# Every second column of the MLP's first weights as a stationary tile, and the second weights' rows to match

## The chip, the cores and the metric

The kernel runs on one core of one Trainium2 chip. The metric is the device time of one execution in microseconds (us), and the three runs shown are compared by their median.

## What is computed

The reference is a decoder trunk of four layers on 256 tokens with 1024 features, in float32. Each layer has a token mixer (latent attention, block-sparse attention, a state-space mixer, latent attention again) and then a dense MLP with a squared ReLU. The part that matters here is the MLP:

```python
def sq_relu_mlp(h, w1, w2):
    a = jax.nn.relu(h @ w1)
    return (a * a) @ w2

for i in range(DEPTH):
    ...
    x = x + m
    x = x + sq_relu_mlp(rmsnorm(x, norm_mlp[i]), mlp_w1[i], mlp_w2[i])
```

`mlp_w1[i]` is 1024 x 4096 and `mlp_w2[i]` is 4096 x 1024. The sum over the 4096 hidden channels does not depend on the order in which they are taken, as long as a column of w1 and a row of w2 with the same number meet.

## The kernel before

All products run on TensorE with each float32 operand split into a high and a low part (`whi`, `wlo` for weights; `hhi`, `hlo` for activations; `uhi`, `ulo` for the hidden values), and three of the four cross products are summed in PSUM. Weights come in units of up to 1 MB, in the order of a list that `plan_mlp` and its sisters write (`units`). SP goes through that list (L2186 to L2203): it waits until the slot's last low split is done, and starts the transfer into one of four slots of `raw`. ScalarE copies a landed unit to `whi` (L557) once TensorE has released the slot; VectorE subtracts to get `wlo` (L573); TensorE waits for that before it uses the unit.

An MLP takes its 4096 hidden channels in 16 chunks of 256. Chunk c has a first-layer unit ("up", columns 256c to 256c+255 of w1, as 8 slabs k of 128 features x 256 columns) and a second-layer unit ("down", rows 256c to 256c+255 of w2, as 2 slabs of 128 rows x 1024 columns). The function `cols` cuts the first, the function `rows` the second; in `rows`, slab k holds the rows 128k to 128k+127 of the unit, one row to a partition.

In the first layer the weights are stationary: a tile m (0 or 1) of 128 hidden channels is loaded for each k, and the 256 tokens are the moving operand. The result lands in PSUM with hidden channels on the partitions. Chunks 0 and 1 of an MLP go through `pe_first_channels` (L841 to L894), with its own high-part loop `first_part` (L855, L856, L861) and the three-product helper `mm3` (L590 to L592). That function also serves the state-space mixer, with keys "dt" and ("cv", 0); `deferred(j)` tells an MLP. Chunks 2 to 15 go through `pe_up` (L974 to L989): for each tile m and each k one product of the high weights with high and low activations side by side (512 moving columns, L982), then for each m and k one product of the low weights with the high activations (256 moving columns, L987).

ScalarE and VectorE turn the PSUM tile into relu, square and its high and low parts (L1027, L1048, L1050, L1032, L1053), always on 128 x 512 elements and element by element. In the second layer the hidden values are stationary, 128 channels of tile k against 128 tokens, and the rows of the down unit's slab k are the moving operand (`pe_out_part`, L902, L903, L906): 24 products of 512 columns for each chunk. Thus slab k of the down unit and tile m = k of the up unit must hold the same channels on the same partitions. TensorE's order is written out in `pe_mlp`: down(c-2), then up(c).

Of the kernel before, what the change touches and what calls it, by code (L numbers as in the profile page):

```python
# [21 lines left out]
P = 128  # L22
SEQ = 256
T = SEQ // P
DM = 1024
KD = DM // P
# [4 lines left out]
CH = 256  # L31
# [71 lines left out]
def build(nc, A, out, stages):  # L103

    ctx = ExitStack()
    with ctx:
# [18 lines left out]
        hflat = hrows[:].rearrange("p k n -> p (k n)")[:, 0:KD * 2 * SEQ].rearrange("p (k a n) -> p k a n", k=KD, a=2)  # L125
        hhi, hlo = hsplit[:, :, 0, :], hsplit[:, :, 1, :]
# [153 lines left out]
        def unit(key, a, b, *srcs):  # L280

            first[key] = len(units)
            view[key] = (0, a, b)
            units.append((a, b, srcs))
# [11 lines left out]
        def rows(w, lo, hi):  # L296
            return w[lo:hi, :].rearrange("(k p) n -> p k n", p=P)

        def cols(w, lo, hi):
            return w[:, lo:hi].rearrange("(k p) n -> p k n", p=P)  # L300

        def used(key):

            return w_used[first[key] % SLOTS], first[key] // SLOTS + 1
# [22 lines left out]
        def plan_mlp(L):  # L327
            w1, w2 = A["mlp_w1"][L], A["mlp_w2"][L]
            for c in range(NCH + 1):
                if c < NCH:  # L330
                    unit(("up", L, c), KD, CH, cols(w1, c * CH, (c + 1) * CH))
                    if c < 2:
                        jobs.add(("up", L, c), ready=used(("up", L, c)))
                    else:
                        b = 0 if jobs.last in (2, 3) else 2
                        up_count[0] += 1
                        for m in range(2):
                            jobs.add(("up", L, c, m), bank=b + m, ready=used(("up", L, c)), freed=(up_added, up_count[0]))
                if c >= 1:
                    unit(("down", L, c - 1), 2, DM, rows(w2, (c - 1) * CH, c * CH))  # L340

        step_unit = {}

# [142 lines left out]
        for j, (kind, L, i) in enumerate(stages):  # L486
            plan_norm(j)
            stage_unit[len(units) + SLOTS + 3] = j
            if kind == "mla":
                plan_mla(j, L, i)  # L490
            if kind == "moba":
                plan_moba(L)
            if kind == "mlp":
                plan_mlp(L)
            if kind == "ssd":
                plan_ssd(L)
# [11 lines left out]
        def hi_lo(key):  # L508
            off, a, b = view[key]
            s = first[key] % SLOTS  # L510
            return (whi[:, s, off:off + a * b].rearrange("p (a b) -> p a b", a=a),
                    wlo[:, s, off:off + a * b].rearrange("p (a b) -> p a b", a=a))

        def wait_unit(te, key):

            te.wait_ge(w_split[first[key] % SLOTS], first[key] // SLOTS + 1)

        def open_job(te, key):

            b, _, _, before = jobs.at[key]  # L520
            if before:
                te.wait_ge(*before)
            return bank[b]
# [64 lines left out]
        def mm3(ps, lhs, rhs, start, stop):  # L588

            nc.tensor.matmul(ps, lhs[0], rhs[0], start=start, stop=False)  # L590
            nc.tensor.matmul(ps, lhs[0], rhs[1], start=False, stop=False)  # L591
            return nc.tensor.matmul(ps, lhs[1], rhs[0], start=False, stop=stop)  # L592
# [44 lines left out]
        def split_input(j):  # L637

            h = hflat if deferred(j) else hsplit
            return h[:, :, 0, :], h[:, :, 1, :]  # L640
# [140 lines left out]
        def deferred(j):  # L781

            return j < len(stages) and stages[j][0] == "mlp"

        def pe_tr(te, j, t, halves=(0, 1)):

            for half in halves:
                if fast(j) and half:
                    te.wait_ge(xn_upper_done, norm_index[j] * T + t - T + 1)
                else:  # L790
                    te.wait_ge(xn_done, 2 * (j * T + t) + half + 1)
                ps = open_job(te, ("tr", j, t, half))
                for k in range(4):
                    kk = 4 * half + k
                    mm = nc.tensor.transpose(ps[:, k * P:(k + 1) * P], xn[:, t, kk * P:(kk + 1) * P], ident[:])  # L795
                mm.then_inc(ready(("tr", j, t, half)), 1)

        def tile_ready(te, j, t, halves=(0, 1)):

            for half in halves:  # L800
                job_copied(te, ("tr", j, t, half))

        def high_ready(te, j, t, half):
            te.wait_ge(h_hi_done, j * 4 + 2 * t + half + 1)
# [36 lines left out]
        def pe_first_channels(te, j, keys):  # L841


            if not deferred(j):
                pe_tr(te, j, 1, [0])
            high_ready(te, j, 1, 0)
            half = KD // 2
            hhi, hlo = split_input(j)

            def first_part(key, items):  # L850
                w, width, ps = hi_lo(key), units[first[key]][1], bank[jobs.at[key][0]]
                for m, k in items:
                    c = slice(m * P, min((m + 1) * P, width))
                    dst = ps[0:c.stop - c.start, m * SEQ:(m + 1) * SEQ]
                    nc.tensor.matmul(dst, w[0][:, k, c], hhi[:, k, :], start=m == 0 and k == 0, stop=False)  # L855
                    nc.tensor.matmul(dst, w[1][:, k, c], hhi[:, k, :], start=False, stop=False)  # L856
                for t in range(T):
                    tile_ready(te, j, t, [0])
                for m, k in items:
                    c = slice(m * P, min((m + 1) * P, width))  # L860
                    nc.tensor.matmul(ps[0:c.stop - c.start, m * SEQ:(m + 1) * SEQ], w[0][:, k, c], hlo[:, k, :],  # L861
                                     start=False, stop=False)

            def part(key, items, last):
                w, width, ps = hi_lo(key), units[first[key]][1], bank[jobs.at[key][0]]
                for m, k in items:
                    c = slice(m * P, min((m + 1) * P, width))
                    mm = mm3(ps[0:c.stop - c.start, m * SEQ:(m + 1) * SEQ],
                             (w[0][:, k, c], w[1][:, k, c]), (hhi[:, k, :], hlo[:, k, :]),
                             m == 0 and k == 0, last and c.stop == width and k == KD - 1)  # L870
                return mm

            def products(key, ms, ks):
                return [(m, k) for m in range((units[first[key]][1] + P - 1) // P) if m in ms for k in ks]

            lower, upper_k = range(half), range(half, KD)
            mlp = keys[0] != "dt"
            for n, key in enumerate(keys):
                wait_unit(te, key)
                open_job(te, key)  # L880
                items = products(key, (0,) if mlp and n else (0, 1), lower)
                if n == 0:
                    first_part(key, items[:6])
                    pe_tr(te, j, 1, [1])
                else:
                    part(key, items[:6], False)
                if items[6:]:
                    part(key, items[6:], False)
            tile_ready(te, j, 0, [1])
            tile_ready(te, j, 1, [1])  # L890
            part(keys[0], products(keys[0], (0, 1), upper_k), True).then_inc(used(keys[0])[0], 1)
            key = keys[1]
            rest = products(key, (0,), upper_k) + products(key, (1,), range(KD)) if mlp else products(key, (0, 1), upper_k)
            part(key, rest, True).then_inc(used(key)[0], 1)  # L894
# [79 lines left out]
        def pe_up(te, L, c):  # L974


            key = ("up", L, c)
            w = hi_lo(key)
            for m in range(2):
                ps = open_job(te, key + (m,))  # L980
                for k in range(KD):
                    nc.tensor.matmul(ps, w[0][:, k, m * P:(m + 1) * P], hflat[:, k].rearrange("p a n -> p (a n)"),  # L982
                                     start=k == 0, stop=False)
            for m in range(2):
                ps = bank[jobs.at[key + (m,)][0]]
                for k in range(KD):
                    mm = nc.tensor.matmul(ps[:, 0:SEQ], w[1][:, k, m * P:(m + 1) * P], hflat[:, k, 0, :], start=False,  # L987
                                          stop=k == KD - 1)
            mm.then_inc(used(key)[0], 1)  # L989

# [1344 lines left out]
```

## Time and profile before

| what | us |
|---|---|
| median of 3 runs | 1312.21 |
| lowest and highest of them | 1311.41, 1316.04 |
| span of the profiled execution, first to last instruction | 1312.0 |
| TensorE busy in it | 1286.5 |
| VectorE busy | 891.4 |
| ScalarE busy | 671.6 |

For the profiled execution the profile gives its span and no device time beside it. "PE" is TensorE's matmuls and "PEld" its loads of stationary tiles, which overlap the matmuls. Recorded durations of matmuls overlap each other too, so the distance between two starts is the time that one takes.

### The profile page before, as it was taken

The numbers are of one execution on the slowest core, as the hardware profiler recorded it, in microseconds if no ns is written. First come the engines' busy times: TensorE is split into PE (matmuls) and PEld (weight loads), VectorE is DVE, ScalarE is ACT, GpSimd is POOL, SyncE is SP. The second block draws the span as 40 slices with busy tenths as digits, with TensorE's granted clock in tenths as the row PEclk, the third lists the DMA queues.
The fourth block names the chain that finished last, engine by engine and source line by source line (L and its number), as shares of the span: only waits on it lengthen the run. The fifth ranks groups of instructions, "written<-read, shape, count | busy, mean of one in ns | idle before, by whom it ended". The sixth has DMA issues, their size and how long they took to land.

```text
span 1312.0 us, 18369 instructions
## 1 busy us (share of the span) xinstructions
PE 1286.5 (98%) x7578; PEld 1126.3 (86%) x7578; DVE 891.4 (68%) x1180; ACT 671.6 (51%) x861; POOL 43.5 (3%) x58
## 2 busy tenths in 40 slices
PE   6999999999999999999999999999999999999998
PEld 5888888888999888887999888888887888888886
DVE  5877666665666666666899886766667876666664
ACT  5555554444555454444776644544445645454442
POOL 3000000000000000000101110000000000000000
PEclk9999999999999999999999999999999999999999
DMA  9744465555845475545574643755554334565540
GB/s 289 143 168 148 141 232 201 193 192 161 233 149 180 132 254 192 192 165 160 181 222 141 203 149 119 249 191 192 191 180 140 117 130 130 168 231 193 192 161 32
DMA packets 146067, 230.93 MB, mean 176 GB/s; under 512 B 7683, under 2 KB 112429, under 8 KB 145984
## 3 DMA queue, kind: packets, MB, share of 16 engines
q1 hardware_dynamic: 143136, 221.66, 50.8%
q0 software_dynamic: 2848, 8.10, 2.9%
q8 instruction: 61, 1.00, 0.3%
q14 instruction: 22, 0.18, 0.0%
HBM read 227.08 MB, written 2.65 MB: 175 GB/s over the span
## 4 chain that ended last, share of the span: by engine, by line
PE 88%; DVE 7%; DMA 1%; issue 1%; ACT 1%; POOL 1%; SPq 0%; POOLq 0%; DVEq 0%; ACTq 0%
PE bank L982 15%; PE acc L902 12%; PE acc L903 12%; PE acc L906 12%; PE bank L987 8%; PE bank L590 7%; PE bank L591 7%; PE bank L592 7%; DVE wlo L573 2%; PE bank L1402 1%; PE bank L1105 1%; PE bank L795 1%; PE bank L1408 1%; PE bank L1090 1%; DMA raw<-in_mla_w_in 1%
## 5 line engine op out<-in xcount | busy, mean ns | idle before, releaser
L573 DVE TENSOR_TENSOR wlo<-raw,whi 128x2048 fp32r<-128x2048 f32 (+2 forms) x207 | 464.7, 2255 | 139.6 <-ACT whi L557 139.5
L557 ACT ACTIVATE whi<-raw 128x2048 fp32r<-128x2048 f32 (+2 forms) x207 | 386.8, 1879 | 45.8 <-PE acc L906 44.2
L982 PE MATMUL bank<-hsplit,whi 128*128 128x512 f32 x896 | 212.2, 389 | 0.0
L903 PE MATMUL acc<-wlo,uhi 128*128 128x512 f32 x512 | 200.1, 391 | 0.0
L902 PE MATMUL acc<-whi,uhi 128*128 128x512 f32 x512 | 199.6, 390 | 0.0
L982 PEld LDWEIGHTS bank<-hsplit,whi 128*128 128x128 f32 x896 | 168.2, 188 | 34.9
L906 PE MATMUL acc<-whi,ulo 128*128 128x512 f32 x512 | 159.2, 390 | 0.0
L590 PE MATMUL bank<-hsplit,whi 128*128 128x256 f32 (+2 forms) x540 | 154.5, 286 | 0.3 <-DVE xn L1980 0.3
L592 PE MATMUL bank<-hsplit,wlo 128*128 128x256 f32 (+2 forms) x540 | 151.4, 280 | 0.0
L591 PE MATMUL bank<-hsplit,whi 128*128 128x256 f32 (+2 forms) x540 | 151.4, 280 | 0.0
L1027 ACT ACTIVATE relu<-bank 128x512 f32<-128x512 f32 x56 | 33.5, 598 | 188.9 <-PE bank L987 188.9
L987 PEld LDWEIGHTS bank<-hsplit,wlo 128*128 128x128 f32 x896 | 114.9, 191 | 4.4
L987 PE MATMUL bank<-hsplit,wlo 128*128 128x256 f32 x896 | 116.2, 283 | 0.0
L906 PEld LDWEIGHTS acc<-whi,ulo 128*128 128x128 f32 x512 | 96.1, 188 | 20.4
L903 PEld LDWEIGHTS acc<-wlo,uhi 128*128 128x128 f32 x512 | 96.4, 188 | 18.2
L902 PEld LDWEIGHTS acc<-whi,uhi 128*128 128x128 f32 x512 | 96.4, 188 | 18.0
L1048 DVE TENSOR_TENSOR relu<-bank,relu 128x512 f32<-128x512 f32 x56 | 38.7, 691 | 96.0 <-ACT relu L1027 96.0
L590 PEld LDWEIGHTS bank<-hsplit,whi 128*128 128x128 f32 (+2 forms) x540 | 100.9, 187 | 1.7 <-issue 1.3
L591 PEld LDWEIGHTS bank<-hsplit,whi 128*128 128x128 f32 (+2 forms) x540 | 100.8, 187 | 0.9 <-issue 0.7
L592 PEld LDWEIGHTS bank<-hsplit,wlo 128*128 128x128 f32 (+2 forms) x540 | 100.7, 187 | 0.0
L1032 ACT ACTIVATE uhi<-rsq 128x512 fp32r<-128x512 f32 x64 | 40.5, 633 | 110.6 <-DVE rsq L1050 81.9
L1053 DVE TENSOR_TENSOR ulo<-rsq,uhi 128x512 fp32r<-128x512 f32 x64 | 44.3, 693 | 47.6 <-ACT uhi L1032 47.6
(252 smaller groups left out, 1813.4 us busy)
## 6 DMA issues: line engine op xcount, KB each, us to landing
raw<-in_mlp_w SPq DMA_DIRECT2D x128, 1024.0 KB, 5.5
raw<-in_ssd_w_in SPq DMA_DIRECT2D x18, 1024.0 KB, 5.4
raw<-in_mla_w_o SPq DMA_DIRECT2D x16, 1024.0 KB, 4.9
raw<-in_mla_w_ukv SPq DMA_DIRECT2D x8, 1024.0 KB, 5.8
raw<-in_moba_w_qkv SPq DMA_DIRECT2D x16, 512.0 KB, 5.3
raw<-in_ssd_w_out SPq DMA_DIRECT2D x8, 1024.0 KB, 4.9
raw<-in_mla_w_uq SPq DMA_DIRECT2D x8, 768.0 KB, 6.0
raw<-in_mla_w_in SPq DMA_DIRECT2D x4, 1024.0 KB, 7.5
```

The source lines that it names most:

```text
L557: nc.scalar.activation(whi[:, s, lo:e], raw[:, s, lo:e], ACT.Copy).then_inc(w_hi_done[s], 1)
L573: nc.vector.tensor_tensor(wlo[:, s, lo:e], raw[:, s, lo:e], whi[:, s, lo:e].bitcast(F32), ALU.subtract).then_inc(w_split[s], 1)
L590: nc.tensor.matmul(ps, lhs[0], rhs[0], start=start, stop=False)
L591: nc.tensor.matmul(ps, lhs[0], rhs[1], start=False, stop=False)
L592: return nc.tensor.matmul(ps, lhs[1], rhs[0], start=False, stop=stop)
L902: nc.tensor.matmul(acc[t][half][:], lh, wh[:, k, n], start=begin and k == 0, stop=False)
L903: nc.tensor.matmul(acc[t][half][:], lh, wl[:, k, n], start=False, stop=False)
L906: mm = nc.tensor.matmul(acc[t][half][:], ll, wh[:, k, n], start=False, stop=end and k == 1)
L982: nc.tensor.matmul(ps, w[0][:, k, m * P:(m + 1) * P], hflat[:, k].rearrange("p a n -> p (a n)"), start=k == 0, stop=False)
L987: mm = nc.tensor.matmul(ps[:, 0:SEQ], w[1][:, k, m * P:(m + 1) * P], hflat[:, k, 0, :], start=False, stop=k == KD - 1)
L1032: nc.scalar.activation(uhi[:, c % 2].rearrange("p a b -> p (a b)"), rsq[:, c % 2, :], ACT.Copy).then_inc(uhi_done, 1)
L1053: nc.vector.tensor_tensor(ulo[:, c % 2].rearrange("p a b -> p (a b)"), rsq[:, c % 2, :], uhi[:, c % 2].rearrange("p a b -> p (a b)").bitca ...
```

## The change

A stationary tile m of a first-layer unit is now every second column, starting at column m (`m::2`), instead of 128 adjacent columns. So partition p of tile m holds channel 2p+m of the chunk. The second-layer unit is loaded so that slab k holds row 2p+k on partition p: a partition takes two adjacent rows. The transfers of the first-layer units stay as they are, and so do all products, their order and their counts. In `pe_first_channels` the new slices hold for MLPs only; for the state-space mixer the expressions give the same slices as before.

```diff
+        def interleaved_rows(w, lo, hi):
+            return w[lo:hi, :].rearrange("(p k) n -> p k n", p=P)
...
-                    unit(("down", L, c - 1), 2, DM, rows(w2, (c - 1) * CH, c * CH))
+                    unit(("down", L, c - 1), 2, DM, interleaved_rows(w2, (c - 1) * CH, c * CH))
...
             def first_part(key, items):
...
-                    c = slice(m * P, min((m + 1) * P, width))
-                    dst = ps[0:c.stop - c.start, m * SEQ:(m + 1) * SEQ]
+                    c = slice(m, width, 2) if deferred(j) else slice(m * P, min((m + 1) * P, width))
+                    dst = ps[0:min(P, width), m * SEQ:(m + 1) * SEQ]
                     nc.tensor.matmul(dst, w[0][:, k, c], hhi[:, k, :], start=m == 0 and k == 0, stop=False)
...
             def part(key, items, last):
...
-                    c = slice(m * P, min((m + 1) * P, width))
-                    mm = mm3(ps[0:c.stop - c.start, m * SEQ:(m + 1) * SEQ],
+                    c = slice(m, width, 2) if deferred(j) else slice(m * P, min((m + 1) * P, width))
+                    mm = mm3(ps[0:min(P, width), m * SEQ:(m + 1) * SEQ],
                              (w[0][:, k, c], w[1][:, k, c]), (hhi[:, k, :], hlo[:, k, :]),
-                             m == 0 and k == 0, last and c.stop == width and k == KD - 1)
+                             m == 0 and k == 0, last and (m + 1) * P >= width and k == KD - 1)
...
         def pe_up(te, L, c):
...
-                    nc.tensor.matmul(ps, w[0][:, k, m * P:(m + 1) * P], hflat[:, k].rearrange("p a n -> p (a n)"),
+                    nc.tensor.matmul(ps, w[0][:, k, m::2], hflat[:, k].rearrange("p a n -> p (a n)"),
                                      start=k == 0, stop=False)
...
-                    mm = nc.tensor.matmul(ps[:, 0:SEQ], w[1][:, k, m * P:(m + 1) * P], hflat[:, k, 0, :], start=False,
+                    mm = nc.tensor.matmul(ps[:, 0:SEQ], w[1][:, k, m::2], hflat[:, k, 0, :], start=False,
                                           stop=k == KD - 1)
```

## Rows read from the trace of the kernel before

**Rows 1.** The page's head and busy times: us, share of the span, instructions.

```profile
span 1312.0 us, 18369 instructions
...
PE 1286.5 (98%) x7578; PEld 1126.3 (86%) x7578; DVE 891.4 (68%) x1180; ACT 671.6 (51%) x861; POOL 43.5 (3%) x58
```

**Rows 2.** The chain that ended last, by engine and by line, shares of the span.

```profile
PE 88%; DVE 7%; DMA 1%; issue 1%; ACT 1%; POOL 1%; SPq 0%; POOLq 0%; DVEq 0%; ACTq 0%
PE bank L982 15%; PE acc L902 12%; PE acc L903 12%; PE acc L906 12%; PE bank L987 8%; PE bank L590 7%; PE bank L591 7%; PE bank L592 7%; DVE wlo L573 2%; PE bank L1402 1%; PE bank L1105 1%; PE bank L795 1%; PE bank L1408 1%; PE bank L1090 1%; DMA raw<-in_mla_w_in 1%
```

**Rows 3.** Stage table, first MLP: us, busy by engine, clock, DMA share, GB/s.

```profile
176.00:326.00 150.00, 150.00 (x768) 128.56 (x767) 91.79 (x72) 68.14 (x57) 0.00 (x0) 1.00 0.61 203
```

**Rows 4.** The chain in order of time, one chunk: start us, us, what.

```profile
187.37 3.63 PE bank L982 x16
191.00 1.91 PE bank L987 x16
192.91 0.23 PE acc L902
...
198.38 0.23 PE bank L982
```

**Rows 5.** Groups by line and shape, matmuls: count, busy us, mean ns, idle before.

```profile
L982 PE MATMUL bank<-hsplit,whi 128*128 128x512 f32 x896 | 212.2, 389 | 0.0
...
L987 PE MATMUL bank<-hsplit,wlo 128*128 128x256 f32 x896 | 116.2, 283 | 0.0
...
L855 PE MATMUL bank<-hsplit,whi 128*128 128x256 f32 x24 | 5.9, 283 | 0.0
```

**Rows 6.** DMA queue of the weights: packets, MB, share of 16 engines.

```profile
q1 hardware_dynamic: 143136, 221.66, 50.8%
```

**Rows 7.** Tile raw, 176 to 320 us: idle (us, times) until; landing times.

```profile
  PE acc L906: 11.1, 11
...
DMA to landing us min/median/max: 4.9/5.5/7.4
```

**Rows 8.** Line L557 over the whole span: idle before it until a transfer.

```profile
  DMA raw<-in_mla_w_uq: 1.0, 1
```

**Rows 9.** Waits of SP's queue: us in total, times, longest.

```profile
SPq L2203 <- DVE wlo L573: 1155.0, 201, 18.2
```

**Rows 10.** Groups by line and shape, loads of stationary tiles; the last has 64 columns.

```profile
L982 PEld LDWEIGHTS bank<-hsplit,whi 128*128 128x128 f32 x896 | 168.2, 188 | 34.9
L987 PEld LDWEIGHTS bank<-hsplit,wlo 128*128 128x128 f32 x896 | 114.9, 191 | 4.4
...
L592 PEld LDWEIGHTS bank<-hsplit,wlo 128*64 128x64 f32 x16 | 2.1, 134 | 0.0
```

**Rows 11.** Timeline of loads before products of one moving column.

```profile
752.98 0.97 PEld L1749 LDWEIGHTS bank<-ones,gss 128*128 128x128 f32 x8
```

**Rows 12.** Timeline of products with 64 stationary columns, first and last of ten.

```profile
29.01 0.28 PE L592 MATMUL bank<-hsplit,wlo 128*64 128x256 f32 x1
...
30.07 0.28 PE L592 MATMUL bank<-hsplit,wlo 128*64 128x256 f32 x1
```

**Rows 13.** Stage table for the L987 products of one chunk, columns as in rows 3.

```profile
191.00:192.91 1.91, 1.91 (x17) 1.91 (x17) 1.20 (x1) 0.00 (x0) 0.00 (x0) 1.00 0.84 207
```

**Rows 14.** Timeline in the block-sparse mixer's first products, first and last of 23.

```profile
343.46 0.28 PE L590 MATMUL bank<-whi,hsplit 128*128 128x256 f32 x1
...
345.95 0.28 PE L591 MATMUL bank<-wlo,hsplit 128*128 128x256 f32 x1
```

**Rows 15.** The chain at an MLP's first products, first and last of 67.

```profile
161.79 0.12 PE bank L592
...
169.71 0.12 PE bank L592
```

**Rows 16.** Timeline of 512-column products early in the span, first and last of ten.

```profile
26.39 0.39 PE L592 MATMUL bank<-whi,hsplit 128*128 128x512 f32 x1
...
28.49 0.39 PE L592 MATMUL bank<-whi,hsplit 128*128 128x512 f32 x1
```

More of the change, by code:

```diff
@@ L859, in first_part @@
                 for m, k in items:
-                    c = slice(m * P, min((m + 1) * P, width))
-                    nc.tensor.matmul(ps[0:c.stop - c.start, m * SEQ:(m + 1) * SEQ], w[0][:, k, c], hlo[:, k, :],
+                    c = slice(m, width, 2) if deferred(j) else slice(m * P, min((m + 1) * P, width))
+                    nc.tensor.matmul(ps[0:min(P, width), m * SEQ:(m + 1) * SEQ], w[0][:, k, c], hlo[:, k, :],
                                      start=False, stop=False)
@@ L866, in part @@
                 for m, k in items:
-                    c = slice(m * P, min((m + 1) * P, width))
-                    mm = mm3(ps[0:c.stop - c.start, m * SEQ:(m + 1) * SEQ],
+                    c = slice(m, width, 2) if deferred(j) else slice(m * P, min((m + 1) * P, width))
+                    mm = mm3(ps[0:min(P, width), m * SEQ:(m + 1) * SEQ],
                              (w[0][:, k, c], w[1][:, k, c]), (hhi[:, k, :], hlo[:, k, :]),
-                             m == 0 and k == 0, last and c.stop == width and k == KD - 1)
+                             m == 0 and k == 0, last and (m + 1) * P >= width and k == KD - 1)
                 return mm
```

## The prediction, made before the changed kernel was run

> **What bounds the kernel now.** I read the busy times first, then the chain of waits, then the stretch in which the change lies, and last the loads of the stationary tiles. In the busy times TensorE is at 98% of the span, no other engine is above 68%, and the weight loads (PEld) stand at 86% [rows 1]. The chain that ended last says the same: 88% of it is TensorE's own work, and the two lines of the first MLP layer, L982 and L987, carry 15% and 8% [rows 2]. So an edit counts only if it changes how fast TensorE is fed, or makes it wait. The clock was granted at full level (2.4 GHz) in the first MLP's stretch [rows 3], and the same in the other three, so no level change enters the sum.
>
> One hidden chunk of an MLP takes 11.01 us on that chain, from 187.37 to 198.38: 16 products of L982 in 3.63 us (227 ns each), 16 of L987 in 1.91 us (119.4 ns each), and 24 of the second layer in 5.47 us (228 ns each) [rows 4]. There is no gap between them, and the chunks repeat: 14 such chunks in each of 4 MLPs are 616 us. The recorded means of 389 and 283 ns [rows 5] are longer than these steps because matmuls overlap; I work with the steps, which are what the time is made of.
>
> **The change, part by part.** It leaves every instruction in place: the same products, splits, copies and transfers, in the same order with the same semaphores. Three things change inside them.
>
> First, the loads of w2. There are 64 second-layer units of 1 MB. Before, each partition takes two separate rows of 4 KB; after, rows 2p and 2p+1, which lie side by side, 8 KB in one piece. That is 128 pieces fewer per unit, 8192 of the 143136 packets of that queue [rows 6], if an 8 KB piece stays one packet. The transfers may land sooner than their 5.5 us median [rows 7]. What that is worth is seen from who waits for them. In a whole MLP stretch the high split on ScalarE (L557) waited 11.1 us for TensorE to release the slot, and for no transfer [rows 7]; over the whole program it waited for a transfer once, 1.0 us, and that one was of the MLA weights [rows 8]. SP's loads themselves wait for the low split on VectorE (1155 us in 201 waits) [rows 9]: the slot's release sets them. I take 0 us. The cover is the time between landing and the slot's turn. If transfers were slower by a microsecond or two, L557 would start later, but TensorE shows no wait in the stretch to pass it on to. Nothing moves past a queue, and no wait is added.
>
> Second, which hidden channel sits on which partition. The first layer's tile m now holds channels 2p+m, and the second layer contracts with row 2p+m. ReLU, square and both splits work element by element, on tiles of the same size: 0 us.
>
> Third, the only edit on the path: the stationary tile of the first layer is read with a step of two elements, 128 values spread over 1024 bytes of a partition where they lay in 512. It touches 896 loads of L982, 896 of L987, 72 of L855, L856 and L861 at full width (24 each, one of the three rows stands) [rows 5], and 312 through the three-product helper (in each of 4 MLPs 32 pairs of channel tile and k, less the 6 of the first part, by 3); that is 2176 loads, of which 896 stand beside 512 moving columns and 1280 beside 256.
>
> What does a load cost now? Recorded, 188 to 191 ns [rows 10]. But loads are pipelined: where the product moves a single column, eight loads took 0.97 us, so the step is (0.97 - 0.19) / 7 = 111 ns [rows 11]. That is the load's own limit, and it is close under the 119.4 ns of L987. With half as many stationary columns the load is recorded at 134 ns [rows 10], and yet nine products of 256 columns took 1.06 us, 118 ns each [rows 12]; so the products, not the loads, set the step now. The slack of a load is about 120 - 111 = 9 ns beside 256 columns and 227 - 111 = 116 ns beside 512.
>
> In the stretch of L987 the loads are shown busy in 1.91 of 1.91 us [rows 13]. Here the Trainium skill (Perfetto Trace Analysis, Identifying the Most-Contended Engine) judges TensorE's headroom by the busy share of the weight loads. By that share L987 would have no headroom, and each nanosecond of a longer load would cost 1280 x 1 ns = 1.3 us at once; by the step of rows 11 the first 9 ns are free.
>
> No row here shows a stationary operand with a step, so its price has to be bounded. Above: half the rate, since twice the bytes are spanned. The load step becomes 222 ns. Beside 512 columns that still hides under 227. Beside 256 columns the step goes from 120 to 222, and 1280 x 102 ns = 131 us. Below: the products' steps vary with the addresses of the two operands, from 113.2 ns (22 steps in 2.49 us) [rows 14] to the 120 ns of the MLP's first products (66 steps in 7.92 us) [rows 15]. If the new addresses fell on the best of these, 1280 x 6.8 ns = 8.7 us would be gained. I take 0, for this reason: while L987 runs, TensorE already takes in 256 moving values, 1024 bytes of a partition, in 120 ns [rows 4], with no more than 13 ns over 256 columns at 2.4 GHz. A load that steps by two spans the same 1024 bytes in the same time. The rate is one that the memory is shown to give to this engine, and the load's own count of 128 values stays as it is.
>
> The Trainium skill (SBUF — State Buffer, worked example of the ports, its note on cachelines) speaks to this by itself: full rate needs two hits on each 16-byte line. Four-byte values at a step of two just meet that, so by the page the price is 0 as well, at the last step but one that it calls free; no run here shows it yet.
>
> **Sum.** 0 (transfers) + 0 (channels) + 0 (loads) on a span of 1312.0 us [rows 1]. The median of the three runs shown is 1312.21 us, 0.2 us above that span, and I take 1312.2 us. What a measurement of this kernel can tell from no change is about 0.5%, 6.6 us.
>
> **The rivals.** (A) Slower, by the load at half rate. Its place is the 1280 loads beside 256 columns; it decides once a load's own step exceeds 120 ns, and it passes 0.5% once the step exceeds 120 + 6.6 us / 1280 = 125 ns. At half rate: 1312.2 + 131 = 1443 us. For it: only 9 ns of slack. Against it: the moving stream above, and that 116 ns of slack cover the other 896 loads. Chance 0.12.
>
> (B) Slightly slower, by collisions of the two reads. Steps depend on addresses: nine 512-column products took 2.10 us, 233 ns each, elsewhere [rows 16], against 227 here, and tile 1 now starts 4 bytes beside tile 0 instead of 512. L982 at 233 gives 896 x 6 ns = 5.4 us; 256-column steps are at the upper end of rows 14 and 15 already. Twice that, since the read spans twice the bytes, and 1 to 2 ns on the 1280 others: up to 14 us, 1326 us; a typical case 1320 us. Chance 0.06.
>
> (C) Faster: the same effect with the other sign, or earlier landings that shorten a stage's end. All of rows 14's advantage: 1312.2 - 8.7 = 1303.5 us. It passes 0.5% only if three quarters of that is gained, and for the landings no waiter is seen. Chance 0.07.
>
> (D) That the change does not do what it says: an 8 KB piece may be cut into two packets again, and then the packets stay at their number. The time is 1312 us either way, so it lies inside the forecast.
>
> **How the numbers follow.** The forecast, no change, holds 0.75; A and B make slower 0.18; C makes faster 0.07. The range reaches from 1304 (nearly all of C) to 1326 (the upper end of B) and leaves out A and little more.
>
> **What would show it.** Right: chunks of 11.0 us on the chain, with 3.63 us for 16 of L982 and 1.91 us for 16 of L987; loads of L982 and L987 at 188 and 191 ns; some 8000 packets fewer, landings of second-layer units shorter, no new waiter. Wrong by A: L987's 16 take 3 us or more while L982's stay near 3.63, and loads are recorded near 300 ns. Wrong by B or C: both steps shift by a few nanoseconds, the same in all 56 chunks. The forecast falls altogether if TensorE is shown to wait in the MLP for a split or a transfer.

## The result, and the profile after

The changed kernel took 1320.78 us (median of 6 runs, 1317.35 to 1323.18) against 1314.26 us for the kernel before on the same chips (6 runs, 1311.41 to 1316.16). The ratio is 1.0047, with a 95% interval of 1.0031 to 1.0063. It is slower by about 6 us: just under the 0.5% that the prediction named as what can be told from no change, but clear of 1 in its interval.

The page's head, busy times and weight queue of the changed kernel answer to [rows 1, 6]. Lines of this kernel stand three further down, so L985 is the old L982, L990 the old L987, and L905, L906, L909 are the old L902, L903, L906.

```profile
span 1315.6 us, 18369 instructions
...
PE 1291.0 (98%) x7578; PEld 1130.4 (86%) x7578; DVE 891.6 (68%) x1180; ACT 671.6 (51%) x861; POOL 43.5 (3%) x58
...
q1 hardware_dynamic: 134944, 221.66, 50.2%
```

The same instructions ran, 18369 of them. The packets fell by 143136 - 134944 = 8192, exactly the number predicted: each pair of rows of w2 now moves as one piece. TensorE is busy for longer, by 4.5 us; VectorE and ScalarE are not. The chain in order of time shows one chunk, beside [rows 4]:

```profile
187.15 3.73 PE bank L985 x16
190.89 1.92 PE bank L990 x16
192.80 0.23 PE acc L905
...
198.27 0.23 PE bank L985
```

A chunk goes from 11.01 to 11.12 us, and all of it is in one line: 16 products of 512 moving columns take 3.73 us where they took 3.63, 233.3 ns each instead of 226.7. The 256-column products of L990 and the second layer keep their steps. Each of the 16 steps is 233 ns, the 8 of tile 0 and the 8 of tile 1 alike (1.87 us for either eight), and it is the same in all 56 chunks: 896 products x 6.6 ns = 5.9 us. The groups of loads and of matmuls, by line and shape, beside [rows 5, 10]:

```profile
L985 PEld LDWEIGHTS bank<-hsplit,whi 128*128 128x128 f32 x896 | 173.0, 193 | 35.7
L990 PEld LDWEIGHTS bank<-hsplit,wlo 128*128 128x128 f32 x896 | 115.5, 195 | 4.5
```

```profile
L985 PE MATMUL bank<-hsplit,whi 128*128 128x512 f32 x896 | 218.1, 394 | 0.0
L990 PE MATMUL bank<-hsplit,wlo 128*128 128x256 f32 x896 | 116.2, 282 | 0.0
```

The loads are recorded 4 to 5 ns longer on both lines. Beside the 512-column products there are still 35.7 us of idle load time before them, 40 ns a load, so by the record no product waited for its load's end; and yet it is these products that became longer, from 389 to 394 ns in the record.

No waiter changed. In the same stretch as [rows 7] ScalarE's split still waited for TensorE and for no transfer, and the transfers landed as late as before, in spite of the larger pieces:

```profile
  PE acc L909: 11.1, 11
...
DMA to landing us min/median/max: 4.7/5.5/7.4
```

The two profiled spans differ by only 3.6 us. 5.9 us came in the MLPs; 2.1 us went the other way between the second and third MLP (from the end of the last L987 group to the first L982 group of the next MLP, 605.84 to 826.70 before and 608.51 to 827.24 after), and the start was 0.3 us earlier. Of the 2.1 us the stage tables tell the cause of most. For the stretch 617 to 645 us the kernel before shows a mean clock of 0.94, a piece of it at the lower level (1.2 GHz) after TensorE's waits at that change of stage; the profiled execution of the changed kernel shows none there. A lack of 0.06 over 28 us is some 1.7 us of full clock. The rest came at 736 us, where TensorE waited for VectorE (L1980) in the kernel before only: from the start of the eight L1765 products there (L1768 in the changed kernel) to the next product 1.37 us passed, against 0.80 in the changed kernel. Neither place is one that the change touches. First the kernel before, then the changed one (columns as in [rows 3]):

```profile
617.00:645.00 28.00, 24.91 (x186) 23.26 (x186) 20.63 (x32) 18.21 (x27) 1.94 (x4) 0.94 0.34 113
```

```profile
617.00:645.00 28.00, 24.91 (x189) 23.15 (x188) 21.44 (x33) 18.35 (x30) 1.67 (x3) 1.00 0.44 141
```

So the loss of the change is the 5.9 us of the MLPs, which is 0.45% and agrees with the timed ratio; a single span is a poor witness for so small a change.

### The profile page after: what moved, and what is told of

It is laid out like the page before. It is cut to its first block, busy times and chain, and to the rows that moved or that the text cites. A ratio compares the mean times of both kernels' runs of the same rounds, so it can differ in the third digit from the quotient of the medians.

```text
span 1315.6 us, 18369 instructions
## 1 busy us (share of the span) xinstructions
PE 1291.0 (98%) x7578; PEld 1130.4 (86%) x7578; DVE 891.6 (68%) x1180; ACT 671.6 (51%) x861; POOL 43.5 (3%) x58
## 3 DMA queue, kind: packets, MB, share of 16 engines
q1 hardware_dynamic: 134944, 221.66, 50.2%
## 4 chain that ended last, share of the span: by engine, by line
PE 90%; DVE 6%; issue 1%; ACT 1%; DMA 1%; POOL 0%; SPq 0%; POOLq 0%; DVEq 0%; ACTq 0%
PE bank L985 16%; PE acc L905 12%; PE acc L906 12%; PE acc L909 12%; PE bank L990 8%; PE bank L593 7%; PE bank L594 7%; PE bank L595 7%; DVE wlo L576 2%; PE bank L1405 1%; PE bank L1108 1%; PE bank L1742 1%; PE bank L798 1%; PE bank L1411 1%; PE bank L1093 1%
## 5 line engine op out<-in xcount | busy, mean ns | idle before, releaser
L985 PE MATMUL bank<-hsplit,whi 128*128 128x512 f32 x896 | 218.1, 394 | 0.0
L985 PEld LDWEIGHTS bank<-hsplit,whi 128*128 128x128 f32 x896 | 173.0, 193 | 35.7
L906 PE MATMUL acc<-wlo,uhi 128*128 128x512 f32 x512 | 200.1, 391 | 0.0
L905 PE MATMUL acc<-whi,uhi 128*128 128x512 f32 x512 | 199.4, 390 | 0.0
L909 PE MATMUL acc<-whi,ulo 128*128 128x512 f32 x512 | 159.3, 390 | 0.0
L990 PEld LDWEIGHTS bank<-hsplit,wlo 128*128 128x128 f32 x896 | 115.5, 195 | 4.5
L990 PE MATMUL bank<-hsplit,wlo 128*128 128x256 f32 x896 | 116.2, 282 | 0.0
L909 PEld LDWEIGHTS acc<-whi,ulo 128*128 128x128 f32 x512 | 96.1, 188 | 20.4
L906 PEld LDWEIGHTS acc<-wlo,uhi 128*128 128x128 f32 x512 | 96.1, 188 | 18.1
L905 PEld LDWEIGHTS acc<-whi,uhi 128*128 128x128 f32 x512 | 96.2, 188 | 18.1
```

The source lines that it names most:

```text
L905: nc.tensor.matmul(acc[t][half][:], lh, wh[:, k, n], start=begin and k == 0, stop=False)
L906: nc.tensor.matmul(acc[t][half][:], lh, wl[:, k, n], start=False, stop=False)
L909: mm = nc.tensor.matmul(acc[t][half][:], ll, wh[:, k, n], start=False, stop=end and k == 1)
L985: nc.tensor.matmul(ps, w[0][:, k, m::2], hflat[:, k].rearrange("p a n -> p (a n)"), start=k == 0, stop=False)
L990: mm = nc.tensor.matmul(ps[:, 0:SEQ], w[1][:, k, m::2], hflat[:, k, 0, :], start=False, stop=k == KD - 1)
```

## The experiments

Each reading below is the chain in order of time, cut to one chunk: start us, us, what. High products are those of the high weights beside 512 columns (L982, L985 in the changed kernel), low products those of the low weights beside 256 columns (L987, L990). The kernel before has 3.63 us for 16 high products and 1.91 for 16 low ones; the changed kernel 3.73 and 1.92. Where no ratio is given a kernel was run once; in every run the sums of 16 steps agree within 2 ns over all 56 chunks, so differences of 0.02 us between kernels can be read.

### Loads or transfers

**loads_only** is the changed kernel with the second-layer units loaded as before.

```diff
-                    unit(("down", L, c - 1), 2, DM, interleaved_rows(w2, (c - 1) * CH, c * CH))
+                    unit(("down", L, c - 1), 2, DM, rows(w2, (c - 1) * CH, c * CH))
```

> Stationary tiles with a step of two, the second-layer units loaded as in the kernel before (so that tile and row no longer hold the same channels). Theory 1 (the strided load meets the 512 moving columns beside it): all of the loss stays, 16 products of L985 in 3.73 us, 11.11 us a chunk, 0.45% over before. Theory 2 (the 8 KB pieces of the transfers disturb TensorE's reads): 3.63 us, 11.01 us a chunk, time as before.

Measured: ratio 1.0042 (1.0026 to 1.0057), and

```profile
188.20 3.73 PE bank L985 x16
191.93 1.92 PE bank L990 x16
```

**rows_only** is the kernel before with the new loads of w2.

```diff
-                    unit(("down", L, c - 1), 2, DM, rows(w2, (c - 1) * CH, c * CH))
+                    unit(("down", L, c - 1), 2, DM, interleaved_rows(w2, (c - 1) * CH, c * CH))
```

> Second-layer units with two adjacent rows per partition, stationary tiles of 128 adjacent columns as before (channels no longer matched). Theory 1: 3.63 us for 16 of L985's counterpart, time within 0.2% of before, some 8200 packets fewer. Theory 2: 3.73 us, 0.45% over before.

Measured: ratio 1.0000 (0.9988 to 1.0011), with the same fall of the packets; chain, then queue (this kernel's lines too stand three further down):

```profile
188.43 3.63 PE bank L985 x16
192.06 1.91 PE bank L990 x16
```

```profile
q1 hardware_dynamic: 134944, 221.66, 50.4%
```

The two halves of the change come apart cleanly. The loads with a step carry the whole loss, and the larger pieces of the transfers are worth nothing either way.

### How far a load reaches

**step_of_four** and **step_of_three** widen the step in `pe_up`, over two slabs; the low product likewise.

```diff
-            w = hi_lo(key)
+            w = [v.rearrange("p k n -> p (k n)") for v in hi_lo(key)]
...
-                    nc.tensor.matmul(ps, w[0][:, k, m::2], hflat[:, k].rearrange("p a n -> p (a n)"),
+                    nc.tensor.matmul(ps, w[0][:, CH * min(k, KD - 2) + m:CH * min(k, KD - 2) + m + 4 * P - 3:4], hflat[:, k].rearrange("p a n -> p (a n)"),
```

> In chunks 2 to 15 the tiles take every fourth value over two slabs (other columns than the reference's). If a load needs time by the bytes that it spans, the load's own step goes from 111 ns to about 222: L990's 16 take 3.6 us instead of 1.91, L985's stay near 3.73 or rise a little. If the load's time goes by its 128 values, L990 stays at 1.91 and L985 rises again by about 0.1 us, to 3.84. If neither matters beyond a step of two, 3.73 and 1.91.

Measured: 1418.85 us; the chain, and the load group of L990:

```profile
190.81 3.76 PE bank L985 x16
194.57 3.62 PE bank L990 x16
```

```profile
L990 PEld LDWEIGHTS bank<-hsplit,wlo 128*128 128x128 f32 x896 | 213.3, 327 | 0.0
```

> The changed kernel, but in chunks 2 to 15 the tiles take every third value over two slabs (other columns than the reference's). If the load's own time goes by the 16-byte pieces that it touches (96, against 64 at a step of two and 128 at a step of four, where L990's step was 226 ns): about 0.75 x 226 = 170 ns, so L990's 16 take about 2.7 us. If it goes by values until the step is four: 1.91 us. L985's 16 in 3.73 to 3.80 us either way.

Measured: 1366.68 us (`3 * P - 2:3` in the diff above), with

```profile
187.99 3.77 PE bank L985 x16
191.75 2.72 PE bank L990 x16
```

```profile
L990 PEld LDWEIGHTS bank<-hsplit,wlo 128*128 128x128 f32 x896 | 163.1, 260 | 0.0
```

Here a load's own time is the limit: 16 low products take 1.92, 2.72 and 3.62 us at steps of two, three and four, 120, 170 and 226 ns in the mean. The first of the 16 steps is short at both wider steps (118 and 122 ns); the other 15 are 174 and 233 ns, and these are the load's own. They are nearly as 3 to 4, which was the expectation by 16-byte pieces touched, 96 and 128 of them, and give some 1.8 ns a piece. The bytes spanned, 1536 and 2048, are as 3 to 4 too, so these runs do not tell pieces from bytes. By that measure an estimate for the 64 pieces of a step of two is 116 ns, just inside the 120 ns of the product beside it. It cannot be carried down to adjacent columns: their 32 pieces would take 58 ns, and the load's own step is 111 [rows 11]. So the prediction's rival A, a load at half rate that costs some 100 ns on each low product, is what a step of four does, not a step of two. But the 512-column products do not follow this: 3.73, 3.77, 3.76 us.

**half_strided** loads 64 columns with a step of two, **half_adjacent** 64 adjacent ones.

```diff
-                    nc.tensor.matmul(ps, w[0][:, k, m::2], hflat[:, k].rearrange("p a n -> p (a n)"),
+                    nc.tensor.matmul(ps[0:64], w[0][:, k, m:P:2], hflat[:, k].rearrange("p a n -> p (a n)"),
...
```

> The changed kernel, but in chunks 2 to 15 a tile loads only 64 columns, every second of 128 (half of the hidden channels are left out there). Theory 1b (the cost goes by the stretch of memory that the load reads: 64 strided values span the 512 bytes that 128 adjacent ones do): L985's 16 take 3.63 us as before the change. Rival (any step of two costs 6.6 ns a product beside 512 columns): 3.73.

```profile
187.89 3.63 PE bank L985 x16
191.52 1.88 PE bank L990 x16
```

> As half_strided, with 64 adjacent columns (half of the hidden channels are left out in chunks 2 to 15). Theory 1b: half the stretch of before, L985's 16 take less than 3.63 us, about 3.58 (another 6.6 ns per two... at most 3.3 ns a product less), or stay at 3.63 if 13 ns over the columns is a floor. Rival: 3.63.

```profile
188.96 3.68 PE bank L985 x16
192.63 1.84 PE bank L990 x16
```

With the step kept and the stretch back at 512 bytes the 3.63 us returned, as theory 1b said: the step as such is not what costs 6.6 ns. The load also takes half as many values here, but that alone does not make a product fast, as half_adjacent shows. There half the stretch did not lower the time; it rose to 3.68 us, which neither theory had. So the cost does not simply grow with the bytes that a load reads, either. 3.63 us is a good case that reads within one even stretch of 512 bytes give, with 128 adjacent values or 64 strided ones. Tile 1 of the strided ones starts 4 bytes into its stretch and is as fast as tile 0 (1.81 us for 8 of either): there a start that is 4 bytes off costs nothing.

### Where the reads start

**adjacent_off_by_one** keeps adjacent columns and moves the tiles' starts, tile 0 one column up and tile 1 one column down.

```diff
-                    nc.tensor.matmul(ps, w[0][:, k, m * P:(m + 1) * P], hflat[:, k].rearrange("p a n -> p (a n)"),
+                    nc.tensor.matmul(ps, w[0][:, k, 1 + 126 * m:1 + 126 * m + P], hflat[:, k].rearrange("p a n -> p (a n)"),
...
```

> In chunks 2 to 15 of each MLP adjacent columns, but tile 0 starts at column 1 and tile 1 at column 127 (other columns than the reference's). If the cost comes of a tile start that is off a 64-byte boundary, L982's 16 take more than 3.63 us, up to 3.73. If it comes of the step of two, 3.63 us within 0.02.

Measured, chain and load group:

```profile
187.57 3.73 PE bank L982 x16
191.30 1.90 PE bank L987 x16
```

```profile
L982 PEld LDWEIGHTS bank<-hsplit,whi 128*128 128x128 f32 x896 | 168.1, 188 | 40.4
```

The same 3.73 us without any step, and with loads recorded at the 188 ns of before. A loss of this size on the products therefore needs no longer load; a load that lies otherwise in memory is enough. That it is the same loss is not shown: the single steps here lie between 227 and 238 ns, where the changed kernel has 233 throughout.

**adjacent_shift64**, **strided_shift64** and **strided_shift128** place the MLP's activations 16 or 32 elements further in their buffer, in the kernel before and in the changed one.

```diff
-        hflat = hrows[:].rearrange("p k n -> p (k n)")[:, 0:KD * 2 * SEQ].rearrange("p (k a n) -> p k a n", k=KD, a=2)
+        hflat = hrows[:].rearrange("p k n -> p (k n)")[:, 16:16 + KD * 2 * SEQ].rearrange("p (k a n) -> p k a n", k=KD, a=2)
```

> The kernel before, with the MLP's activations placed 64 bytes further, so that the moving operand and the next tile's load no longer start on the same 64-byte place within 256 bytes. Theory 1 (the step of a product goes by how the next load's addresses stand to those of the moving columns beside it; in the trace of before, 256-column products with a load displaced by 64 bytes step in 113 to 117 ns instead of 120): L982's 16 go from 3.63 to 3.73 us, as with the step of two, and L987's 16 fall from 1.91 to about 1.82. Rival (the step of two costs by itself, whatever the addresses): 3.63 and 1.91 stay.

```profile
189.55 3.68 PE bank L982 x16
193.23 1.81 PE bank L987 x16
...
200.51 3.68 PE bank L982 x16
```

> The changed kernel, with the MLP's activations placed 64 bytes further. Theory 1: the two steps move, L985's 16 somewhere between 3.63 and 3.78 us and L990's between 1.82 and 1.95, not both at 3.73 and 1.91. Rival: 3.73 and 1.91 as without the shift.

```profile
188.59 3.73 PE bank L985 x16
192.33 1.92 PE bank L990 x16
...
199.74 3.73 PE bank L985 x16
```

> The changed kernel, with the MLP's activations placed 128 bytes further. Theory 1: as for 64 bytes, possibly with other values. Rival: 3.73 and 1.91.

```profile
187.96 3.70 PE bank L985 x16
191.66 1.94 PE bank L990 x16
```

With adjacent columns the shift moved both steps: the high products lost half of what was expected, the low ones gained what was expected, and a chunk came to 10.96 us. With the step of two the chunk came to 11.15 us with 64 bytes and 11.10 with 128, against 11.12 without a shift. At 64 bytes the rival's values stood; at 128 both steps moved a little, to 3.70 and 1.94, as theory 1 had allowed. Neither shift brings the 3.63 us back.

Three runs asked which address decides. **both_off_by_one** starts the tiles one column later (all but the last of the 16, which has no room) and the activations 4 bytes later; **adjacent_shift4** moves the activations alone (`[:, 1:1 + KD * 2 * SEQ]`); **adjacent_shift128** moves them by 128 bytes (32 elements).

```diff
+            def at(m, k):
+                lo = min(CH * k + P * m + 1, UNIT - P)
+                return slice(lo, lo + P)
...
-                    nc.tensor.matmul(ps, w[0][:, k, m * P:(m + 1) * P], hflat[:, k].rearrange("p a n -> p (a n)"),
+                    nc.tensor.matmul(ps, w[0][:, at(m, k)], hflat[:, k].rearrange("p a n -> p (a n)"),
...
```

> The kernel before with adjacent columns, tiles starting one column later (in chunks 2 to 15, other columns than the reference's) and the MLP's activations placed 4 bytes further as well, so that load and moving columns stand to each other as before, both off by 4 bytes. If the distance between the two addresses decides: 3.63 us for L982's 16, as before. If a load that does not start on a 16-byte (or 64-byte) place costs by itself: 3.73, as in adjacent_off_by_one.

```profile
186.56 3.80 PE bank L987 x16
190.36 1.97 PE bank L992 x16
...
197.82 3.80 PE bank L987 x16
```

> The kernel before with only the MLP's activations placed 4 bytes further. If the distance decides: 3.73 us, as in adjacent_off_by_one, whose distance has the same size. If the load's own start decides: 3.63.

```profile
189.27 3.80 PE bank L982 x16
193.07 1.95 PE bank L987 x16
...
200.46 3.80 PE bank L982 x16
```

> The kernel before with the MLP's activations 128 bytes further. If distances below 256 bytes spread the reads: L982's 16 between 3.63 and 3.73 us, L987's 16 near 1.81, as with 64 bytes. If 64 bytes was a place of its own: 3.63 and 1.91.

```profile
189.09 3.73 PE bank L982 x16
192.81 1.90 PE bank L987 x16
...
200.19 3.73 PE bank L982 x16
```

None of the outcomes written down beforehand for these three runs came. The distance between the two addresses does not decide by itself: kept the same, with both 4 bytes off, the high products take 3.80 us (in this kernel's lines L987 and L992 are the two products). The activations' own 4 bytes give the same 3.80, more than the tile's (3.73); these two are the worst of all. A shift of 128 bytes gives 3.73 and none of the gain of 64. What rule of the memory stands behind these steps stays open; the runs show that they depend on where both reads start and how far the load reaches, in steps between 3.63 and 3.80 us for the high products.

### A version that beats both

Two kernels put only the low parts of the first-layer units elsewhere in their slots, to take the low products' gain and leave the high ones alone. The mixer's small tile `kp` moves into a stage's memory to make room. The products' lines stand two further down, L984 and L989.

```diff
-        wlo = sb("wlo", [P, SLOTS, UNIT], F32R)
+        wlo = sb("wlo", [P, SLOTS, UNIT + 64], F32R)
...
+        low_at = {first[key]: 16 for key in first if isinstance(key, tuple) and key[0] == "up"}
...
-                nc.vector.tensor_tensor(wlo[:, s, lo:e], raw[:, s, lo:e], whi[:, s, lo:e].bitcast(F32),
+                nc.vector.tensor_tensor(wlo[:, s, d + lo:d + e], raw[:, s, lo:e], whi[:, s, lo:e].bitcast(F32),
...
```

> The kernel before, with only the low parts of the first-layer units placed 64 bytes further within their slots (and room made for it by 256 bytes more per slot). Theory 1: L982 keeps 3.63 us for 16, L987 falls from 1.91 to about 1.82 (16 x 6 ns), a chunk from 11.01 to 10.91, and a third of the first products gain 6 ns each: 56 x 0.096 + 128 x 0.006 = 6.1 us less than before, ratio about 0.995. Rival: no change, ratio 1.000.

Measured: ratio to before 0.9984 (0.9971 to 0.9997), and a chunk of 10.98 us:

```profile
190.54 3.63 PE bank L984 x16
194.16 1.89 PE bank L989 x16
...
201.52 3.63 PE bank L984 x16
```

> As adjacent_low_shift64, with the low parts 192 bytes further. Theory 1 (the addresses of load and moving columns decide): the load now stands to the moving columns as in adjacent_shift64, so L987's 16 take 1.81 us while L982's keep 3.63; 0.10 us a chunk and up to 0.8 us in the first products, some 6 us under before, ratio about 0.9955. Rival (the shift of all activations helped for another reason): 1.89 us as with 64 bytes, ratio 0.998 to 0.999.

Measured (48 in place of 16): ratio 0.9999 (0.9989 to 1.0009).

```profile
186.51 3.63 PE bank L984 x16
190.14 1.89 PE bank L989 x16
...
197.53 3.62 PE bank L984 x16
```

The low products gained 0.02 us a chunk and not 0.10, at either place, so theory 1 in its simple form, that the distance between load and moving columns sets the step, fell here as it did in both_off_by_one. The wider slots also changed where every low part lies, by 256 bytes more from slot to slot; that was not tried by itself. With 192 bytes even that little was lost again in the second layer, and a chunk took 11.02 us. The shift of all activations was then timed:

> The same kernel as adjacent_shift64, timed. Its chunks add up to 143.21 us a stretch against 143.77, so 4 x 0.56 = 2.2 us less than before: ratio 0.998, and 0.994 against the changed kernel. If the single run's 1312.0 us was chance alone, ratio 1.000.

Measured: 1312.16 us (12 runs) against 1313.89 for before, ratio 0.9984 (0.9972 to 0.9995), as its chunks had foretold. Against the changed kernel that is 0.9984 / 1.0047 = 0.9937, from two comparisons. So two versions of the kernel before, without the change, come out 0.16% under it: the one with its MLP activations 64 bytes further and adjacent_low_shift64. The timed runs do not tell them apart; by its chunk the first is ahead, with 10.96 against 10.98 us.

## Why the prediction was wrong

**The bound was read rightly.** TensorE's chain sets the time, and the loss came out of TensorE's steps, in the stretch and the lines named.

**The transfers at 0 us: right, and shown.** 8192 packets fewer and rows_only at a ratio of 1.0000. The shorter landings that were to go with it did not come, and nothing waited for them.

**The channels at 0 us: right.** ScalarE's and VectorE's busy times are those of before, to 0.2 us.

**The strided load at 0 us: wrong.** This is the step that failed. The argument was that a load with a step of two spans 1024 bytes in the time in which TensorE also takes in 1024 bytes of moving values, and that 116 ns of slack cover the 896 loads beside 512 columns. The first half held: L990's step stayed at 120 ns, where only 9 ns of slack were seen, so the load did not become slower to any degree that mattered. So [rows 11], by which the first 9 ns are free, judged these loads rightly, and the full busy share of [rows 13] did not: the loads were recorded 4 ns longer and the step did not move. The second half did not follow. Slack covers a load that ends late; here it did not keep the product beside the load from becoming longer. The cost appeared just where the slack was largest, 6.6 ns on each of the 896 products of 512 columns, 5.9 us. The sum held no term for that: its 0 for the loads asked only whether a load comes in time. Why these products became longer the runs do not show.

**Rival B was the right one in place and size, and had too small a chance.** It named L982 at 233 ns and 896 x 6 ns = 5.4 us; measured were 233.3 ns and 5.9 us. [rows 16] already showed the kernel's own 512-column products at 233 ns elsewhere, and [rows 14, 15] showed 256-column products between 113 and 120 ns in the same span: steps of one shape differed within the span with no wait to explain it, and the kernel's 227 ns was at the good end of what was seen. An edit that moves the addresses on the bound line had more to lose than to gain, and 0.06 for the loss against 0.07 for a gain did not say so. Its details were not right. It pointed at tile 1's start 4 bytes beside tile 0, but tile 0's products are as slow as tile 1's (233 ns), and in half_strided, with the same start, both are fast. Its sign was that both steps shift, and L990's did not. That its typical case of 1320 us lies so near the measured 1320.78 is in part luck: it is 8 us over a kernel before of 1312.2, where the loss was 6 us over one of 1314.26.

**What can be told from no change** was put at 0.5%. Six runs on either side told 0.47% from nothing.

**Rival A was refuted for a step of two** and shown for a step of four (3.62 us for 16 low products).

The note on cachelines in the Trainium skill (SBUF — State Buffer, Door 1: The DMA port swizzle) asks for two hits on each 16-byte line. The low products' means agree: 120 ns at a step of two, as before the change, and 170 and 226 ns at steps of three and four. Its other wording, that four-byte values stay free up to a step of four, does not agree with the 226 ns here. The whole loss lay elsewhere, in the products beside the loads.

## What to carry to other kernels

When TensorE is the bound, read the step between its products, not the recorded durations, and compare the same shape in different places of the trace. Where the steps differ and the engine waits for nothing, the layout of its operands can be part of the time, as it was here, and an edit of an access pattern on that line can cost even where the loads themselves keep up. A load that is hidden is not thereby free for what it is hidden beside: here it cost 6.6 ns a product. Larger pieces of a transfer were worth nothing here, where no one waited for it.

## What the runs showed that was not expected

- Moving the activations of an MLP by 4 bytes costs 16 high products 0.17 us (3.63 to 3.80) and a chunk 0.18 us, with the same instructions; moving them by 64 bytes gains 0.05 us a chunk, by 128 bytes costs 0.09.
- Loading half as many stationary columns did not make the products faster: 64 adjacent columns gave 3.68 us, 64 strided ones 3.63.
- A load's recorded duration (188 ns) was the same in the good and in one bad case (adjacent_off_by_one); only the distance between the products' starts told them apart.
